# One more order for a hybrid decoder layer: first weight pieces, GpSimd's halves, an output half on ScalarE, and new sequences for three engines

## The reference

```
u  = rms_norm(h, norm_mix);  z = u @ w_in                        # 1024 -> 1792 + 1536
y1 = rwkv7_time_mix(z[:, :1792], ...)                            # 8 heads x 64, a recurrence over tokens
y2 = moba_attention(q, k, v of z[:, 1792:])                      # 8 heads x 64, causal, one block of 256
h  = h + concat(y1, y2) @ w_mix_out
h  = h + memory_cross_attention(rms_norm(h), rms_norm(mem), w_xq, w_xkv, w_xo)   # 4 heads x 256
h  = h + square(relu(rms_norm(h) @ w_ff1)) @ w_ff2               # 4096 hidden
out = rms_norm(h, norm_final)
```

## Time and profile before

| | |
|---|---|
| median of 3 runs | 469.25 us (468.83 to 470.98) |
| the profiled execution | 469.52 us, span of its records 467.7 us |
| busy: PE, PE's weight loads | 449.5, 400.3 us |
| busy: DVE, ACT, POOL | 317.1, 246.0, 35.1 us |
| read from HBM | 71.35 MB, 155 GB/s over the span |
| granted TensorE clock | 0.998 over the span |

### The profile page before, as it was taken

One profiled execution on the slowest core, in us unless ns is written; L12 is line 12 of the kernel. 1 busy time (PEld: TensorE's weight loads), 2 busy tenths in 40 slices (PEclk: granted clock), 3 DMA queues, 4 the chain that ended last, 5 costly groups with the idle time before them and its releaser, 6 DMA issues.

```text
span 467.7 us, 10247 instructions
## 1 busy us (share of the span) xinstructions
PE 449.5 (96%) x4342; PEld 400.3 (86%) x4342; DVE 317.1 (68%) x477; ACT 246.0 (53%) x395; POOL 35.1 (8%) x54
## 2 busy tenths in 40 slices
PE   4999989998999999999999999999999999999994
PEld 3999989986889888997999998888888888888883
DVE  2867999991669759479557484775848475756665
ACT  5999943343555365444544365553626454445344
POOL 8300000000000000017000006200000000000000
PEclk9999999999999999999999999999999999999999
DMA  7964525125332243553543365258374565758312
GB/s 255 323 207 141 181 90 175 32 88 167 96 114 91 91 143 127 177 185 96 175 131 127 106 192 169 90 179 270 107 253 155 206 200 160 228 184 265 131 47 90
DMA packets 58912, 73.04 MB, mean 156 GB/s; under 512 B 1378, under 2 KB 46516, under 8 KB 58868
## 3 DMA queue, kind: packets, MB, share of 16 engines
q1 hardware_dynamic: 57684, 71.08, 47.2%
q10 hardware_dynamic: 1104, 1.05, 0.7%
q0 software_dynamic: 80, 0.26, 0.3%
HBM read 71.35 MB, written 1.05 MB: 155 GB/s over the span
## 4 chain that ended last, share of the span: by engine, by line
PE 77%; DVE 6%; issue 2%; ACT 1%; ACTq 0%
PE bank L532 10%; PE bank L548 8%; PE bank L549 7%; PE bank L550 7%; PE bank L585 6%; PE bank L587 6%; PE bank L586 6%; PE bank L530 6%; PE bank L565 2%; PE bank L566 2%; PE bank L567 2%; PE bank L529 2%; PE bank L910 2%; PE bank L931 1%; DVE w_lo L1318 1%
## 5 line engine op out<-in xcount | busy, mean ns | idle before, releaser
L1318 DVE TENSOR_TENSOR w_lo<-raw,w_hi 128x1024 fp32r<-128x1024 f32 x128 | 155.5, 1235 | 58.5 <-ACT w_hi L994 58.2
L994 ACT ACTIVATE w_hi<-raw 128x1024 fp32r<-128x1024 f32 x128 | 132.6, 1054 | 56.1 <-PE bank L550 26.0
L548 PE MATMUL bank<-op,w_hi 128*128 128x256 f32 x416 | 121.3, 291 | 0.2 <-ACT w_hi L994 0.2
L549 PE MATMUL bank<-op,w_hi 128*128 128x256 f32 x416 | 117.6, 283 | 0.0
L550 PE MATMUL bank<-op,w_lo 128*128 128x256 f32 x416 | 117.6, 283 | 0.0
L548 PEld LDWEIGHTS bank<-op,w_hi 128*128 128x128 f32 x416 | 79.6, 191 | 2.7 <-issue 1.0
L532 PE MATMUL bank<-op,w_hi 128*128 128x512 f32 x224 | 80.0, 396 | 0.0
L549 PEld LDWEIGHTS bank<-op,w_hi 128*128 128x128 f32 x416 | 79.7, 192 | 0.2
L550 PEld LDWEIGHTS bank<-op,w_lo 128*128 128x128 f32 x416 | 79.6, 191 | 0.0
L530 PE MATMUL bank<-op,w_lo 128*128 128x256 f32 x256 | 66.3, 279 | 0.0
L530 PEld LDWEIGHTS bank<-op,w_lo 128*128 128x128 f32 x256 | 48.3, 189 | 2.5
(11 more groups left out here) (253 smaller groups left out, 575.2 us busy)
## 6 DMA issues: line engine op xcount, KB each, us to landing
raw<-in_w_ff SPq DMA_DIRECT2D x32, 1024.0 KB, 5.5
raw<-in_w_in SPq DMA_DIRECT2D x12, 1024.0 KB, 5.9
raw<-in_w_xkv SPq DMA_DIRECT2D x8, 1024.0 KB, 5.7
raw<-in_w_mix_out SPq DMA_DIRECT2D x4, 1024.0 KB, 4.9
raw<-in_w_xq SPq DMA_DIRECT2D x4, 1024.0 KB, 5.2
raw<-in_w_xo SPq DMA_DIRECT2D x4, 1024.0 KB, 4.9
xval<-in_x SPq DMA_DIRECT2D x4, 256.0 KB, 5.1
raw<-in_w_in ACTq DMA_DIRECT2D x4, 256.0 KB, 6.9
```

Source lines behind the costliest of these rows:

```text
L548: mm(dst, wh[:, k, :], op_hi[which][:, k, :], start=first, stop=False)
L549: mm(dst, wh[:, k, :], op_lo[which][:, k, :], start=False, stop=False)
L994: op(view(w_hi), r, ACT.Copy).then_inc(hi_done, 1)
L1318: tt(view(w_lo), r, view(w_hi).bitcast(f32), ALU.subtract).then_inc(lo_done, 1)
```

## The change

Four edits go together.

1. ACT starts all four pieces of the first unit, and then loads the square root's table. Before, the table load stood after the second piece.
2. POOL adds the two halves of `square_sum` in one more instruction of 128 x 256. `rms(2)` and `rms(3)` on PE lose one of two matmuls for each result.
3. The output half (1,0) is started by ACT itself, after it has ended it. SP starts the other three.
4. The three lists are new. Of the lists only two lines are shown.

```diff
-                if i == 2:
-                    act.wait_ge(pool_const, 1)
-                    op(small[:, 15:16], eps[:, 0:1], ACT.Sqrt)
                 k = slice(2 * i, 2 * i + 2)
                 act.dma_start(first_to[:, k, :], first[:, k, UNITS[0][3]:UNITS[0][3] + 256]).then_inc(first_in[i], 16)
+            act.wait_ge(pool_const, 1)
+            op(small[:, 15:16], eps[:, 0:1], ACT.Sqrt)
...
                     last = nc.gpsimd.tensor_tensor(square_sum, square_sum, square, ALU.add)
-                    if j < 3:
-                        link(last)
-                last.then_inc(pool_square, 1)
+                    link(last)
+                nc.gpsimd.tensor_tensor(square_sum[:, 0, :], square_sum[:, 0, :], square_sum[:, 1, :],
+                                        ALU.add).then_inc(pool_square, 1)
...
                 if i == 2:
-                    for a in range(2):
-                        last = mm(B[5][:, 0:T], ones[:, :], square_sum[:, a, :], start=(a == 0), stop=(a == 1))
+                    last = mm(B[5][:, 0:T], ones[:, :], square_sum[:, 0, :], start=True, stop=True)
...
                     for n in range(NT):
-                        for a in range(2):
-                            last = mm(B[3][:, n:n + 1], square_sum[:, a, tokens_of(n)], ones[:, 0:1],
-                                      start=(a == 0), stop=(a == 1))
+                        last = mm(B[3][:, n:n + 1], square_sum[:, 0, tokens_of(n)], ones[:, 0:1], start=True, stop=True)
...
                 for j, done in enumerate((act_final, dve_final)):
+                    if (n, j) == (NT - 1, 0):
+                        continue
...
+                act.wait_ge(act_final, NT)
+                act.dma_start(out.rearrange("b (n p) d -> p (b n) d", p=128)[:, NT - 1, 0:512],
+                              ostage[:, NT - 1, 0:512]).then_inc(out_done, 16)
...
-            dense(8); lora(); dense(6); key_sums(); dense(4); spread(1); dense(3); load(1, 0); dense(7)
+            spread(0); dense(9); lora(); dense(5); spread(1); key_sums(); dense(16); load(1, 0); load(1, 1)
...
-            outq(0, 0); dense(2); outq(0, 1); outq(0, 2); outq(0, 3); dense(2); outq(1, 0); outq(1, 1)
+            dense(1); solve(0); solve(1); solve(2); solve(3); pair_scores(0); dense(1); outq(0, 0); outq(0, 1)
+            outq(0, 2); dense(4); outq(0, 3); outq(1, 0); outq(1, 1); outq(1, 2); outq(1, 3); dense(1)
```

More of the change, by code:

```diff
@@ L945, in _ @@
-            pair_turn(2, 1); dense(1); pair_values(2); dense(1); pair_scores(3); state(4); dense(3); state(5)
-            dense(1); state(6); pair_turn(3, 0); pair_turn(3, 1); states_out(); dense(1); pair_values(3)
-            deviation(); dense(1); gate(); dense(32); rms(2); dense(4); scores(0); dense(4); scores(1); turn(0)
-            dense(2); values(0); dense(1); turn(1); scores(2); dense(2); values(1); dense(1); turn(2); scores(3)
-            dense(2); values(2); turn(3); dense(1); values(3); dense(13)
+            params(0); load(0, 0); load(0, 1); load(0, 2); dense(1); load(0, 3); dense(2); params(1); dense(1)
@@ L950, in _ @@
+            pair_turn(3, 1); states_out(); dense(2); deviation(); dense(4); pair_values(3); gate(); dense(28)
+            rms(2); dense(3); scores(0); dense(3); scores(1); turn(0); dense(2); values(0); turn(1); dense(1)
+            scores(2); dense(2); values(1); dense(1); turn(2); scores(3); dense(2); values(2); turn(3); dense(1)
+            values(3); dense(13)
             dense(4)
@@ L1263, in finish @@
                     op(out_half, out_half, ACT.Copy, scale=root[:, n:n + 1]).then_inc(act_final, 1)
-            load(0, 0); load(0, 1); stats(0); load(0, 2); load(0, 3); copies(0); split(); copies(1); split()
-            split(); follow(0); split(); stats(1); split(); gates(); follow(1); split(); split(); split()
-            follow(2); rates(); key_sums(); split(); split(); follow(3); split(); key_norm(); split(); follow(4)
-            split(); decays(); follow(5); split(); keys(2); load(1, 0); split(); load(1, 1); follow(6); split()
@@ new lines, in _ @@
+            load(0, 0); load(0, 1); load(0, 2); stats(0); load(0, 3); split(); split(); copies(0); follow(0)
+            split(); copies(1); split(); split(); follow(1); stats(1); gates(); split(); follow(2); split()
+            split(); rates(); split(); key_sums(); split(); split(); follow(3); key_norm(); split(); split()
+            follow(4); decays(); split(); follow(5); keys(2); split(); follow(6); split(); split(); split()
+            load(1, 0); tokens(); split(); split(); load(1, 1); bonus(); right(0); right(1); split(); right(2)
@@ L1733, in _ @@
             params(0); load(0, 0); load(0, 1); load(0, 2); diagonal_of(0); load(0, 3); params(1); split()
-            spread_copy(0); take(0); split(); split(); split(); follow(0); take(1); split(); follow(1); take(2)
-            split(); follow(2); split(); take(3); split(); sums(); follow(3); split(); diagonal_of(1); split()
-            split(); take(4); keys(0); split(); follow(4); split(); spread_copy(1); take(5); keys(1); reads()
-            split(); keys(2); keys(3); follow(5); tails(0); tails(1); take(6); split(); weighted(); tokens()
@@ new lines, in _ @@
+            spread_copy(1); split(); split(); take(4); keys(0); split(); follow(4); split(); take(5); keys(1)
+            split(); follow(5); keys(2); split(); take(6); keys(3); split(); tails(0); tails(1); reads()
+            weighted(); tokens(); take(7); load(1, 0); follow(6); split(); bonus(); load(1, 1); split(); split()
+            split(); take(8); masked(0); mats(0); mats(1); invert(0); invert(1); invert(2); invert(3); masked(1)
+            invert(4); invert(5); take(9); split(); invert(6); load(1, 2); split(); take(10); join(); load(1, 3)
```

77 lines of the change are left out of this document (37 added, 40 removed).

## The result

| | before | after |
|---|---|---|
| median of 5 runs each, on the same chip | 469.64 us (468.83 to 471.74) | 474.1 us (473.39 to 476.56) |
| ratio | 1 | 1.0106, 95% interval 1.0084 to 1.0128 |
| the profiled execution | 469.52 us | 474.10 us, span 472.1 us |

The changed kernel is slower by 1.1%. The prediction said 466.4 us, and the time lies outside its range. It equals the figure of the rival called *Slower*, but that rival's two pauses of 4.4 us are not what the profile shows.

The account below looks back on a forecast made before the run. PE was taken as the bound, busy 449.5 of 467.7 us. Terms 0.6 + 1.15 + 0.5 + 0.7 + 0.25 - 0.3 = 2.9 us won gave 466.4 us, range 464.7 to 469.0 us.

Parts of the forecast that it names:

- Slower: Rival, chance 0.06: weights ahead of both instruction packets make each pause 4.4 us, giving 474.1 us.
- outq and psi: Term for PE's pauses in these runs: 1.1 us against 1.6 before, 0.5 us won; bounds 1.6 won, 2.0 lost.
- the run of five: Five outq blocks in succession, 480 instructions in 2.6 us: a packet border among them, stopping PE up to 1.8 us.
- Small new waits: Term for new waits around `state(2)`, `pair_turn(1, 1)` and `spread(1)`: 0.3 us lost, from 0 to 1.4.
- The opening: Term for the reordered start: unit 1's first matmul at 18.0 instead of 18.60 us, 0.6 us won.
- The wait at `tokens`: PE's wait for `tails` on DVE: to shrink from 1.4 to some 0.3 us, with `tails` done at 67.7 us.
- The wait at `cross`: PE's wait for `invert`'s fifth part on DVE: at most 0.9 us, with `cross` starting at about 94.6 us.
- the lead: PE's claimed gain by `cross`: about 1.75 us, 0.6 from the opening and 1.15 from 20 to 96 us.
- three signs of being wrong: A pause over 2 us in the five-block run, a new DVE wait over 1 us (30-70 us), `cross` after 95.5.
- The end: Term for the last output halves, started earlier and beside each other by two engines: 0.25 us won, 0 to 0.4.
- `rms(2)`: Half its matmuls go, with two more quarters covering POOL's sum: 0.7 us won together with `rms(3)`, 0.4 to 0.9.

Follow-up runs that it names:

- e10: Changed kernel, with weight units 8 to 21 each started only when the unit before has arrived: 474.0 us, ratio 1.0088.
- e3: Changed kernel, with weight units 8 to 17 loading only one row block of eight or four (light loads, output wrong): 470.19 us, ratio 1.0007.
- e14: Changed kernel with the same partial weight loads as e3 and psi ordered as before: 470.35 us, ratio 1.0007.
- e15: Changed kernel with outq and psi set among the quarters as before, the rest of the new lists kept: 477.89 us, ratio 1.0175.
- e1: Changed kernel with the three lists of before, so only edits 1 to 3: 469.53 us, ratio 0.9987.
- e8: Changed kernel up to `gate`, with the three lists of the kernel before from there on: 476.59 us, ratio 1.0153.
- e9: Kernel before with edits 1 to 3 and only the new order of the opening on PE and ACT: 468.82 us, ratio 0.9985.
- e16: e9 with weight units 8 to 17 loaded only in part (output wrong): 467.06 us, ratio 0.9946.
- e5: Changed kernel with 128 more satisfied waits ahead of PE's first instruction, moving packet borders by 64 instructions: 483.12 us, ratio 1.0284.
- e7: Changed kernel with the long runs of small matmuls in outq and psi broken up by quarters: 479.08 us, ratio 1.0188.
- e13: e12 with weight units 8 to 21 started one at a time: 471.07 us, ratio 1.002.
- e12: e9 with the six quarters within and behind outq set one by one among its blocks: 472.94 us, ratio 1.0055.

## Why the prediction was wrong

**What a packet needs.** The trace has the start of each packet, and PE's instructions can be counted to its border. Counted so, with PE's waits among the instructions, all 45 pauses called issue of over 0.15 us between 60 and 165 us in the 18 profiles stand at a count of 192 more than a multiple of 256, which is a packet's border. I worked out for each packet when PE passed the instruction 309 ahead of the border (the "known" moment below). The 309 is fitted, not known: with it the promptest packets of every profile start 1.0 to 1.2 us behind that moment. Of the packets with no weights in front some six in ten start within 1.5 us; the others come later, some by several us, and why is open:

```
kernel, matmuls ahead    known   packet moves       PE stops  goes on
after, 846               82.18   86.50 to 87.62     87.2      88.95
e10, 846                 82.15   83.64 to 84.59     no stop
after, 2115              126.92  130.95 to 132.22   132.2     133.64
e3 (light), 2115         125.53  129.00 to 130.42   129.9     131.57
e14 (light), 2242        131.16  132.31 to 133.58   133.4     135.01
e15, 2242                135.03  138.25 to 139.23   137.3     140.58
```

PE goes on 1.1 to 1.4 us after the packet's end (up to 1.7 over all 45 pauses). Packets that follow closely start 3.5 us apart and more, in a few cases 3.2. Four blocks of outq are 387 matmuls and weight loads in 2.05 us, so a run uses up 256 instructions in 1.4 us. The row of e14 shows a run outrunning its packet: the packet starts promptly, 1.15 us behind the known moment, and lets PE go on 3.85 us behind it, but the end of psi and the start of a quarter had used up the 309 instructions in 2.3 us, and PE stopped for 1.6. Weights in front add to this (after, 846: 4.3 us from the known moment to the packet's start). In the two rows of 2115 neither is enough: PE took 5.2 us (after) and 4.3 us (e3) for the 309 instructions, more than the 3.85 that e14's prompt packet needed, but the packets started 4.0 and 3.5 us behind the known moment. In the changed kernel the packet before had started 3.8 us earlier; in e3 it had 5.3 us earlier and no weights moved, so what held this one is open.

**The step that failed** is the one on *outq and psi*: that of the new order's borders only the one in the run of five would stop PE, for up to 1.8 us, and that 0.5 us would be won. Measured are 3.4 us more of pauses (5.0 against 1.6). That is 3.9 of the 7.7 us between the forecast and the measured time; the new waits are 2.4 of them and the clock 1.3. I had placed the border's risk by the runs' length alone, had worked with one packet's wait, and had not counted where the other borders fall, though the counts 1607 and 2115 of the earlier trace rows and the order would have told it. Of the five pauses one is in that run (0.6 us), one in psi (1.5 us), one each in the matmuls of `pair_values(0)` (0.9 us) and in a quarter right behind psi (0.2 us), and the largest in the quarter behind the 128 small matmuls of `mats(1)` (1.8 us), where I had seen no risk. These 128 matmuls with their weight loads use up a packet's 256 instructions in 1.4 us (82.16 to 83.57), just as the run of outq does, and the packet behind them had weights in front. The run of five, where I had put the risk, lost the least but one. The bound that I gave this term, 2.0 us lost, was passed by 1.4 us.

**A term was missing**: the fall of the clock behind a pause, 1.3 us. It isn't the new order's alone. In the 20 executions of the kernel before that ran beside e1, seven have a mean granted clock of 0.993 to 0.995 and take 471.2 to 471.98 us, the other thirteen have 0.996 to 0.999 and take 468.96 to 470.08. The executions whose profiles are compared here differ in it too (0.998 before, 0.994 after).

**Small new waits**, put at 0.3 us, measured 2.7 us: 0.7 at `spread(1)`, where I had named the place and was 0.8 us out in the time (the diagonal behind the scan, which `spread(1)` needs, was done at 41.23 us, and I had said 40.5), and 2.0 us more for `w_lo` and the mix stage's operands (2.7 against 0.7), where the last ten halves before `rms(2)` stand in another order among DVE's long operations. e8 bears this out for `w_lo`: with the older order the 1.4 and 0.7 us are 0.7 again. It doesn't for the operand's 0.6 us, which stayed; their cause is not shown.

**Right by mechanism.** The opening: unit 1 starts at 18.09 us (18.0 foretold), 0.5 us won; but e9's and e16's times can't tell it from nothing. The wait at `tokens` shrank by 0.6 us, where 1.1 was foretold: `tails` was done at 68.4 us instead of the 67.7 that I had worked out. The wait at `cross` went altogether, but not by the lead: the pause of 1.8 us ahead of it made PE late, and `cross` began at 96.75 us. Of the prediction's three signs of being wrong this is the one that came. e10, which has no pause there, shows what the lead was worth: 0.5 us of waits for DVE up to `cross` instead of 0.9. The end: from the last matmul's end (466.40 us, before 461.78) to that of the span 5.7 us instead of 5.9, 0.2 won. `rms(2)` won 0.43 us behind its cover; of `rms(3)` nothing arrives: from the start of `rms(2)` to the last matmul it is 237.48 us, and 240.79 before, less two quarters (2.92) and 0.43, is 237.44.

**The sum by what was measured**, against the profiled execution of before: -0.5 (opening) -1.5 (`tokens`, `cross`) +0.7 (`spread`) +3.4 (pauses) +1.3 (clock) +2.0 (`w_lo`, operands) -0.4 (rms) -0.2 (end) = +4.8 us; the two executions lie 4.58 us apart. The pauses and the waits are read from the profiles, the clock's price is the estimate above. That the measured 474.1 us is the figure of *Slower* is luck: that rival had 8.8 us of pauses and no other loss.

**The rule of the Trainium skill** (Runtime: NRT & Kernel Launch, section Instruction fetch mechanics) that crossing a block's border is mostly hidden holds for most of the changed kernel's borders (34 packets) and not for five of them. The block of 256 instructions agrees with the counts 127 matmuls apart and with the move by 64 instructions in e5.

**What stays open.** How long a pause will be can't be told from the order of the instructions alone: e8 and the changed kernel have the same instructions to 180 us, and 6.7 and 5.0 us of pauses. Why the clock fell behind some pauses (1.3 us in e1, 1.7 in e3) and not behind others (1.27 us before, 1.6 in e14), and behind the same pause of 1.76 us in e7 and e8 but not in the changed kernel, is not settled. Light loads leave 2.9 us between the two orders, the larger part of the 4.5 us between their medians with full loads. The pause in psi (1.7), the clock behind it (1.3) and the 2.0 us of waits for DVE, less the gains, come to that by the profiles; only the first was tested, and it moved and did not vanish. A version of the new order with no pause at all was not found.

## What to carry to other kernels

Count an engine's instructions to the borders of its packets before moving runs of short ones: a run that uses up a packet in 1.4 us, where packets come some 3.5 us apart, can stop the engine even when the packet starts promptly (1.6 us in e14). It needn't: a run of four blocks went without a pause before, and with light loads the run of five did. Time won upstream of such a border can be lost at it, since the packet doesn't come earlier by as much (in e10 PE stood at a border 1.4 us earlier and the packet started 0.8 us earlier), and so the effect of an order can't be summed from its waits alone. A saved matmul is worth something only with cover for the work that it is handed to: 0.43 us with two more quarters ahead of `rms(2)`, nothing without. And to break up a run isn't free: each further change between a quarter and a block cost some 0.35 us in e13.

## What the runs showed of the hardware

A pause of TensorE can cost more than its length. In 12 of the 18 profiles the granted clock fell to 0.50 before the last matmul, for 3.4 us, or 6.8 us, and the 12 matmuls of a quarter then took 0.21 us each instead of 0.12. In ten of the twelve it fell during a pause of 1.2 to 5.1 us or up to 2.1 us behind it, in e12 behind a wait of 1.1 us for DVE, in e16 in the opening. 128 satisfied waits ahead of the first matmul made TensorE's first matmul start at 8.93 us instead of 2.39. How far a kernel's executions lie apart goes with the clock more than with the pauses: e7 ran from 475.07 us (clock 0.999) to 481.56 us (0.987), while e5, whose pauses are the longest, ran from 482.48 to 484.29 (0.982 to 0.988), and the kernel before beside them from 469.16 to 471.64.
